# Overflow blocks of a mixture-of-experts layer moved behind their expert's first products, gathered two blocks and transposed one block ahead

## The chip, the cores and the metric

One core of one Trainium2 chip. The metric is the device time of one execution in microseconds (us), here the median of several.

## What is computed

One layer of a hybrid encoder trunk, 512 tokens of width 1024, float32: a mixer (gated DeltaNet beside chunked attention) and a layer norm, and then the part that the change is in, a mixture of 64 experts (gate-up weights 1024 x 512, down weights 256 x 1024) of which every token takes six, one shared expert, and a second layer norm:

```python
def moe_ffn(x, router_w, router_bias, w_gate_up, w_down, ws_gate_up, ws_down):
    scores = jax.nn.sigmoid((xt @ router_w).astype(jnp.float32))
    _, sel = lax.top_k(scores + router_bias.astype(jnp.float32), TOP_K)
    ...
    def block_fn(args):
        tok, wt, e = args
        gu = x_pad[tok] @ w_gate_up[e]
        h = jax.nn.silu(gu[:, :EXPERT_DIM]) * gu[:, EXPERT_DIM:]
        return (h @ w_down[e]) * wt[:, None]
    ...
    routed = jax.ops.segment_sum(y_rows.reshape(n_rows, D), row_tok, num_segments=N + 1)[:N]
    gus = xt @ ws_gate_up
    shared = (jax.nn.silu(gus[:, :SHARED_DIM]) * gus[:, SHARED_DIM:]) @ ws_down
    return (routed.astype(x.dtype) + shared).reshape(B, T, D)
```

## The kernel before

The phases before `experts_phase` (mixer, first layer norm, router, lists of tokens by expert) are not touched. `experts_phase` has one instruction stream per engine, tied by semaphores.

**Blocks.** Each expert works on a block of 64 token rows. Tokens beyond 64 of one expert go to overflow blocks of 64 rows, numbered j; `over_from` says which of them belong to which expert. How many there are depends on the data, so each engine reads two entries of `over_from` at each expert (`later_blocks`, L1622) and branches: `later(i, s)` is its overflow part, skipped or run once per block.

**Turns and steps.** A turn is 8 steps (`STEPS`), a step is one expert, e = 8i + s. There are 8 turns: the first and the last are written out, the six between are one hardware loop per engine (TensorE's is L1854). Step s of TensorE (`turn`):
- `later(i, s)`: overflow blocks of this expert;
- `gate_up(i, s)` (products L1765): 32 matmuls into bank `ps[k % 2]`, with k = s % 4 the weight buffer, incrementing `gu_psum[k]`;
- `transposes` (L1757): four transposes of gathered rows for a later pair of experts, into `ps[2]` or `ps[3]`, copied out by VectorE (L1911, `gathered_xT`);
- `down(i, s - 1)` (products L1772): the down products of the expert before, incrementing `y_psum`;
- `hidden(i, s)` (L1810): transpose of the hidden tile that ScalarE (silu, L1882) and VectorE (L1916) made, incrementing `h_psum[k]`.

In turn 0 the shared expert's down products (L1831) stand in the first four steps.

**One overflow block** (`later` of TensorE, L1778 to L1794), all in bank 5 (`shared`): wait for the expert's gate-up and down weights, for the scatter of the block before (`over_free`) and the gathered rows (`over_gathered`); eight products with the identity (L1786) that transpose `over_x`; VectorE copies them out (`over_xT`, L1924); gate-up products; silu on ScalarE (L1870), multiply on VectorE; transpose (L1792); copy on ScalarE (L1872); down products; ScalarE copies the result to `over_y` (L1875); GpSimd scatter-adds it (L1714) and gathers the next block's rows (L1696) as soon as the transposes have read this one's.

**Weights.** `wgu` and `wdn` have four buffers each: 2 MB of gate-up weights (two DMAs of 1024 KB) and 1 MB of down weights for an expert. The first four experts are loaded earlier. SP then issues, in this order and one behind the other: gate-up of buffer s once `gu_psum[s]` says that its products are done (L2067), down of buffer s - 1 once `y_psum[s - 1]` does (L2073).

Of the kernel before, what the change touches and what calls it, by code (L numbers as in the profile page):

```python
# [1541 lines left out]
def experts_phase(nc, mem, T, ps, x1_rows, sums, w_down, ln_g, ln_b, out):  # L1542
# [67 lines left out]
    blank_word = at("blank_word", [P, 1], "qkT", 1632)  # L1610
# [14 lines left out]
    with nc.Block() as block:  # L1625

        @block.sync
        def _(sp):
            with sp.Fori(1, NE // GROUP) as i:

                for s in range(GROUP + 1):
                    if s < GROUP:
                        T["load_gu"](sp, s, GROUP * i + s, lambda: sp.wait_ge(gu_psum[s], i))
# [21 lines left out]
        def _(pool):  # L1655
# [45 lines left out]
            def later(i, s, alone):  # L1701
                start, end = later_blocks(pool, i, s)
                with pool.If(start < end):
                    with pool.Fori(start, end) as j:
                        pool.wait_ge(over_xt_psum, j + 1)
                        gather_later(j + 1, j + 1)
# [3 lines left out]
                        pool.wait_ge(over_y, j + 1)  # L1710
                        nc.gpsimd.tensor_copy(col2_o[:, :], row_idx[:, bass.ds(j + NE, 1)]).then_inc(over_col2, 1)
                        pool.wait_ge(blank, 1)
                        pool.wait_ge(over_col2, j + 1)
# [17 lines left out]
            gather_later(0, 1, True)  # L1731
            turn(0, first=True)
# [3 lines left out]
            nc.gpsimd.memset(blank_word[:, :], 0.0).then_inc(over_added, 1)  # L1736
# [3 lines left out]
            pool.wait_ge(over_gathered, 16 * blocks + 16)  # L1740
# [6 lines left out]
        def _(pe):  # L1747
# [28 lines left out]
            def later(i, s):  # L1776
                start, end = later_blocks(pe, i, s)
                with pe.If(start < end):  # L1778
                    with pe.Fori(start, end) as j:
                        k, now = block_at(i, s)  # L1780
                        pe.wait_ge(gu_in[k], GU_PARTS * 16 * now)
                        pe.wait_ge(dn_in[k], 16 * now)
                        pe.wait_ge(over_free, 16 * j + 16)
                        pe.wait_ge(over_gathered, 16 * j + 16)
                        for c in range(KC):
                            mm = nc.tensor.matmul(shared[:, c * BLK:(c + 1) * BLK], xo[:, c * P:(c + 1) * P],  # L1786
                                                  ident[0:BLK, 0:BLK], start=True, stop=True)
                        mm.then_inc(over_xt_psum, 1)
                        pe.wait_ge(over_xt_ready, j + 1)
                        gate_up_products(shared, xoT, k, slice(0, BLK)).then_inc(over_gu_psum, 1)  # L1790
                        pe.wait_ge(over_h, j + 1)
                        nc.tensor.transpose(shared[:, 0:P], h_o[:, :], ident[:, :]).then_inc(over_h_psum, 1)  # L1792
                        pe.wait_ge(over_ht, j + 1)
                        down_products(shared, hT_o, k).then_inc(over_y_psum, 1)  # L1794

# [40 lines left out]
            def turn(i, first=False, last=False):  # L1836
                for s in range(STEPS):
                    later(i, s)
# [268 lines left out]
```

## Time and profile before

| | us |
|---|---|
| median of 3 runs | 1496.49 (1493.37 to 1501.87) |
| the profiled execution | 1497.2 |
| its span | 1495.5 |
| TensorE busy, of the span | 87% |
| mean clock granted to TensorE | 0.936 of full speed |
| experts phase, first gate-up product to last down product | 839.3 to 1454.7 |

The page gives an engine's busy time in tenths for 40 equal slices of the span, one digit a slice of 37.4 us; DMA is the mean busy share of 16 DMA engines. A saturated stretch reads slightly above 1. A row of the timeline has start, duration, engine, line, operation and count, and in brackets how long the engine stood idle before it and what it waited for. PE is TensorE's matmuls, PEld its weight loads, PEldq its instruction queue, SPq the queue of SyncE, which issues the weight loads. "issue" means that no cause in the profile explains the idle time.

### The profile page before, as it was taken

What the parts mean: (1) busy time and instruction counts of PE and PEld (TensorE: products, weight loads), DVE (VectorE), ACT (ScalarE), POOL (GpSimd) and SP (SyncE); (2) the same over time, 40 slices, a digit from 0 to 9 for tenths busy, and PEclk for the clock granted to TensorE, in tenths of its full rate; (3) what the DMA queues carried; (4) which work ended last, traced back from release to release, by engine and by line L of the source; (5) the groups of instructions that cost most, each with busy time, mean ns of one, the idle gap of its engine ahead of it and who ended that gap; (6) DMA issues with size and microseconds to landing.
All of it is one profiled execution on the core that took longest, in us unless ns stands there. A gap on an engine that the chain in (4) does not pass through costs nothing. (4 is left out here: it accounts for less than half of the span.)

```text
span 1495.5 us, 23252 instructions
## 1 busy us (share of the span) xinstructions
PE 1303.4 (87%) x8245; PEld 783.0 (52%) x8246; DVE 450.5 (30%) x892; ACT 309.7 (21%) x825; POOL 282.3 (19%) x355
## 2 busy tenths in 40 slices
PE   6999999999998988999999689978787958878680
PEld 5455556555653446888558445544444535444340
DVE  1545544554424442333248211111010101111006
ACT  1222333133312342222231001101011101111020
POOL 2201110111014202000000223323222313322132
PEclk8999999999998998999999899989888979989895
DMA  4441121124001204335821689999999996799874
GB/s 116 119 144 49 44 61 49 43 56 140 0 1 28 57 1 127 98 95 166 348 88 71 220 292 373 342 398 386 403 368 374 384 402 246 288 375 392 341 227 174
DMA packets 134583, 294.87 MB, mean 197 GB/s; under 512 B 12928, under 2 KB 82688, under 8 KB 117968
## 3 DMA queue, kind: packets, MB, share of 16 engines
q1 hardware_dynamic: 117824, 265.72, 47.6%
q0 software_dynamic: 15552, 25.46, 7.2%
q10 hardware_dynamic: 1104, 2.16, 0.4%
q8 instruction: 83, 1.36, 0.3%
q14 instruction: 20, 0.16, 0.0%
HBM read 278.57 MB, written 27.04 MB: 204 GB/s over the span
## 5 line engine op out<-in xcount | busy, mean ns | idle before, releaser
L1765 PE MATMUL bank<-expert_gu,gathered_xT 128*64 128x256 f32 x2048 | 250.8, 400 | 71.1 <-issue 56.0
L1765 PEld LDWEIGHTS bank<-expert_gu,gathered_xT 128*64 128x64 f32 x2048 | 167.4, 144 | 143.5 <-issue 81.2
L427 PE MATMUL bank<-xT,w_head 128*128 128x512 f32 x480 | 241.0, 612 | 1.2 <-PEq L85 1.2
L1916 DVE SCALAR_TENSOR_TENSOR hidden<-gate,slot_w,bank 128x128 f32<-128x128 f32 x64 | 22.2, 347 | 431.7 <-ACT gate L1882 431.7
L1772 PE MATMUL bank<-expert_down,hiddenT 128*64 128x512 f32 x512 | 123.9, 604 | 0.6 <-issue 0.6
L1685 POOL DMA_INDIRECT sum_rows<-expert_y,row_col x64 | 101.4, 1584 | 49.4 <-POOL row_col L1680 47.0
L427 PEld LDWEIGHTS bank<-xT,w_head 128*128 128x128 f32 x480 | 78.8, 190 | 48.5 <-issue 42.4
L1882 ACT ACTIVATE gate<-bank 128x128 f32<-128x128 f32 x64 | 17.8, 278 | 317.6 <-PE bank L1765 317.6
L605 POOL TENSOR_TENSOR LO<-LT_diagonal,level_blocks 128x256 f32<-128x256 f32 x48 | 38.2, 829 | 233.1 <-DVE LT_corner L771 233.1
L1402 DVE TENSOR_TENSOR w_lo<-w_tile,w_hi 128x1024 fp32r<-128x1024 f32 (+1 forms) x32 | 35.2, 1101 | 116.4 <-ACT w_hi L1302 116.4
L1680 POOL COPY row_col<-row_idx 128x1 int32 (+1 forms) x64 | 12.3, 192 | 293.4 <-ACT expert_y L1888 289.5
L1888 ACT COPY expert_y<-bank 128x512 f32<-128x512 f32 x63 | 36.9, 586 | 137.7 <-PE bank L1772 137.7
L1202 PE MATMUL bank<-xh,w_hi 128*128 128x512 f32 x128 | 51.0, 399 | 9.1 <-DVE w_lo L1402 9.1
L1772 PEld LDWEIGHTS bank<-expert_down,hiddenT 128*64 128x64 f32 x512 | 31.5, 136 | 47.6 <-issue 47.4
L717 DVE SCALAR_TENSOR_TENSOR by_channel<-bank,head_taps,by_channel 128x511 f32<-128x511 f32 (+2 forms) x72 | 53.9, 748 | 2.3
L1302 ACT CAST w_hi<-w_tile 128x1024 fp32r<-128x1024 f32 (+1 forms) x32 | 30.3, 946 | 117.1 <-PE bank L1202 110.5
L1202 PE MATMUL bank<-xl,w_hi 128*128 128x512 f32 x128 | 50.8, 397 | 0.0
L1202 PE MATMUL bank<-xh,w_lo 128*128 128x512 f32 x128 | 50.7, 396 | 0.0
L1757 PE MATMUL bank<-ident,gathered_x 128*128 128x128 f32 x256 | 42.6, 291 | 8.4 <-PEq L85 8.4
L1383 POOL COPY tok_col<-tok_idx 128x1 int32<-128x1 int32 x4 | 0.8, 192 | 255.5 <-DVE tok_idx L1532 255.4
L1911 DVE COPY gathered_xT<-bank 128x512 f32<-128x512 f32 x64 | 43.9, 686 | 8.9 <-PE bank L1757 8.9
L1757 PEld LDWEIGHTS bank<-ident,gathered_x 128*128 128x128 f32 x256 | 27.6, 143 | 32.4 <-issue 32.4
(325 smaller groups left out, 1911.0 us busy)
## 6 DMA issues: line engine op xcount, KB each, us to landing
expert_gu<-in_expert_w_gate_up_dram SPq DMA_DIRECT2D x128, 1024.0 KB
expert_down<-in_expert_w_down_dram SPq DMA_DIRECT2D x64, 1024.0 KB
w_head<-in_w_in_dram SPq DMA_DIRECT2D x32, 512.0 KB, 3.9
w_tile<-in_w_in_dram SPq DMA_DIRECT2D x16, 512.0 KB, 4.0
sum_rows<-zero_rows SPq DMA_DIRECT2D x2, 2048.0 KB, 11.7
w_tile<-in_w_branch_a_dram SPq DMA_DIRECT2D x8, 512.0 KB, 5.7
w_pair<-in_w_in_dram SPq DMA_DIRECT2D x6, 512.0 KB
x_rows<-in_x_dram SPq DMA_DIRECT2D x4, 512.0 KB
```

The lines of the kernel that those rows point to most:

```text
L427: mm = nc.tensor.matmul(bank[:, :], w_head[:, g, c, :], xT[:, c, :], start=(c == 0), stop=(c == KC - 1))
L605: nc.gpsimd.tensor_tensor(LO[:, l, :, :], LTd[:, :, :], all_packed(level[:, l, :]), ALU.mult).then_inc(loff_ready[l], 1)
L717: nc.vector.scalar_tensor_tensor(out=ch[:, g, k:SEQ], in0=bank[:, 0:SEQ - k], scalar=w, in1=ch[:, g, k:SEQ], op0=ALU.mult, op1=ALU.add).th ...
L1202: mm = nc.tensor.matmul(ps[4 * p + k][:, :], w[:, c, :].bitcast(F32R), x[:, c, :].bitcast(F32R), start=(c == 0 and part == 0), stop=(c == ...
L1302: nc.scalar.copy(w_hi[:, k % 2, 0:n, :].bitcast(F32R), w_t[:, k * KC:k * KC + n, :]).then_inc(hi_ready[p][k], 1)
L1402: nc.vector.tensor_tensor(w_lo[:, k % 2, 0:n, :].bitcast(F32R), w_t[:, k * KC:k * KC + n, :], w_hi[:, k % 2, 0:n, :], ALU.subtract).then_i ...
L1685: nc.gpsimd.indirect_dma_start(out=sums[s % 2][:, :], out_offset=bass.IndirectOffsetOnAxis(ap=col2[:, k:k + 1], axis=0), in_=y[:, k, :], i ...
L1757: mm = nc.tensor.transpose(ps[2 + a][:, c * P:(c + 1) * P], xg[:, q, chunk * P:(chunk + 1) * P], ident[:, :])
L1765: mm = nc.tensor.matmul(bank[parts[a], 0:2 * P], x[:, c, part], halves[:, a, :, :], start=(c == 0), stop=(c == KC - 1))
L1772: mm = nc.tensor.matmul(bank[parts[a], :], hidden_t[:, c * BLK:(c + 1) * BLK], wdn[k][:, c, a * (D // 2):(a + 1) * (D // 2)], start=(c == ...
L1888: nc.scalar.copy(y[:, b, :], ps[6 + b % 2][:, :]).then_inc(y_ready[b], 1)
L1911: nc.vector.tensor_copy(xgT[:, q % 2, a * KC // 2:(a + 1) * KC // 2, :], ps[2 + a][:, :].rearrange("p (c n) -> p c n", n=P)).then_inc(xt_r ...
```

## The change

1. TensorE runs `later` behind `gate_up` and `transposes` of the same step instead of ahead of them; ScalarE behind its silu of the step, VectorE behind its multiply and its copy of the step. The wait for gate-up weights in `later` goes, since `gate_up` has made it; the wait for down weights moves to the down products.
2. The transposes of block j + 1 are made inside block j, between gate-up and the hidden transpose, in bank 2 or 3, whichever the step leaves free; VectorE copies them at the end of its part. Block 0's are made in the first step. The first of the eight stays a product with the identity, the others become transposes.
3. GpSimd gathers two blocks ahead: rows of blocks 0 and 1 ahead of turn 0, then block j + 2 inside block j.
4. TensorE does not wait for `over_free` (the scatter) any more, but for `over_y` (ScalarE's copy).
5. SP reloads a gate-up buffer at `h_psum[s]` (hidden transpose) instead of `gu_psum[s]`, since the overflow products now read it after the expert's own.
6. `over_y` and `over_col2` count one more from the start.

```diff
@@ sync
-                        T["load_gu"](sp, s, GROUP * i + s, lambda: sp.wait_ge(gu_psum[s], i))
+                        T["load_gu"](sp, s, GROUP * i + s, lambda: sp.wait_ge(h_psum[s], i))
@@ gpsimd
-                        pool.wait_ge(over_xt_psum, j + 1)
-                        gather_later(j + 1, j + 1)
+                        pool.wait_ge(over_xt_psum, j + 2)
+                        gather_later(j + 2, j + 2)
...
             gather_later(0, 1, True)
+            nc.gpsimd.memset(blank_word[:, 1:2], 0.0).then_inc(over_y, 1)
+            nc.gpsimd.memset(blank_word[:, 2:3], 0.0).then_inc(over_col2, 1)
+            pool.wait_ge(over_xt_psum, 1)
+            gather_later(1, 1)
             turn(0, first=True)
@@ tensor
+            def over_transposes(bank):
+                nc.tensor.matmul(bank[:, 0:BLK], xo[:, 0:P], ident[0:BLK, 0:BLK], start=True, stop=True)
+                for c in range(1, KC):
+                    mm = nc.tensor.transpose(bank[:, c * BLK:(c + 1) * BLK], xo[:, c * P:(c + 1) * P], ident[0:BLK, 0:BLK])
+                mm.then_inc(over_xt_psum, 1)
...
                     with pe.Fori(start, end) as j:
-                        k, now = block_at(i, s)
-                        pe.wait_ge(gu_in[k], GU_PARTS * 16 * now)
-                        pe.wait_ge(dn_in[k], 16 * now)
-                        pe.wait_ge(over_free, 16 * j + 16)
-                        pe.wait_ge(over_gathered, 16 * j + 16)
-                        for c in range(KC):
-                            mm = nc.tensor.matmul(shared[:, c * BLK:(c + 1) * BLK], xo[:, c * P:(c + 1) * P],
-                                                  ident[0:BLK, 0:BLK], start=True, stop=True)
-                        mm.then_inc(over_xt_psum, 1)
+                        pe.wait_ge(over_y, j + 1)
                         pe.wait_ge(over_xt_ready, j + 1)
                         gate_up_products(shared, xoT, k, slice(0, BLK)).then_inc(over_gu_psum, 1)
+                        pe.wait_ge(xt_ready[2 * (q % PAIRS) + a], i + (q // PAIRS + 1))
+                        pe.wait_ge(over_gathered, 16 * j + 32)
+                        over_transposes(ps[2 + a])
                         pe.wait_ge(over_h, j + 1)
                         nc.tensor.transpose(shared[:, 0:P], h_o[:, :], ident[:, :]).then_inc(over_h_psum, 1)
+                        pe.wait_ge(dn_in[k], 16 * now)
                         pe.wait_ge(over_ht, j + 1)
                         down_products(shared, hT_o, k).then_inc(over_y_psum, 1)
+                        pe.wait_ge(over_xt_ready, j + 2)
@@ tensor, turn
-                    later(i, s)
...
                         transposes(i + q // PAIRS, q % PAIRS, s % 2)
+                    if first and s == 0:
+                        pe.wait_ge(over_gathered, 16)
+                        over_transposes(shared)
+                    later(i, s, last)
```

The queue of TensorE in one step of the loop, before (`expert_gu_2333` and `expert_down_2337` are the buffers of this expert, `expert_down_2336` that of the expert before; TENSOR_LOAD and ISA read the bounds of the overflow loop, COMPARE_AND_BRANCH skips it):

```order
L1778 COMPARE_AND_BRANCH
L1779 UNCONDITIONAL_BRANCH
...
L1786 MATMUL bank<-ident,over_x 128x64 x8
...
L1765 MATMUL bank<-expert_gu_2333,over_xT 64x256 x16
L1792 MATMUL bank<-ident,over_hidden 128x128
L1772 MATMUL bank<-expert_down_2337,over_hiddenT 64x512 x4
...
L1765 MATMUL bank<-expert_gu_2333,gathered_xT 64x256 x16
L1757 MATMUL bank<-ident,gathered_x 128x128 x4
...
L1772 MATMUL bank<-expert_down_2336,hiddenT 64x512 x4
L1810 MATMUL bank<-ident,hidden 128x128
```

And the same step now:

```order
L1769 MATMUL bank<-expert_gu_2333,gathered_xT 64x256 x16
L1761 MATMUL bank<-ident,gathered_x 128x128 x4
L1622 TENSOR_LOAD over_from
...
L1791 COMPARE_AND_BRANCH
...
L1769 MATMUL bank<-expert_gu_2333,over_xT 64x256 x16
L1797 ISA
L1781 MATMUL bank<-ident,over_x 128x64
L1783 MATMUL bank<-ident,over_x 128x64 x7
L1800 MATMUL bank<-ident,over_hidden 128x128
...
L1776 MATMUL bank<-expert_down_2337,over_hiddenT 64x512 x4
...
L1776 MATMUL bank<-expert_down_2336,hiddenT 64x512 x4
L1820 MATMUL bank<-ident,hidden 128x128
```

The expert's own gate-up and the usual transposes now stand ahead of the register loads, the branch and the block, and the other expert's down products behind them.

## Rows read from the trace of the kernel before

**Rows 1.** The page, busy tenths of the DMA engines in 40 slices

```profile
DMA  4441121124001204335821689999999996799874
```

**Rows 2.** Windows: length, busy of PE, PEld, DVE, ACT, POOL; clock, DMA share, GB/s

```profile
893.00:1443.00 550.00, 451.50 (x2986) 254.53 (x2984) 61.41 (x128) 66.72 (x192) 155.07 (x193) 0.90 0.96 362
944.00:1102.00 158.00, 126.98 (x829) 71.56 (x827) 17.64 (x37) 18.83 (x55) 44.62 (x56) 0.89 1.03 392
1234.00:1242.00 8.00, 7.64 (x53) 3.81 (x53) 0.95 (x2) 1.13 (x3) 1.76 (x2) 1.00 0.39 140
1250.00:1262.00 12.00, 10.74 (x78) 5.45 (x76) 1.29 (x3) 2.16 (x6) 2.21 (x4) 1.00 0.41 118
1278.00:1290.00 12.00, 11.64 (x86) 6.30 (x85) 0.95 (x2) 1.89 (x5) 3.56 (x4) 1.00 0.28 90
1412.00:1422.00 10.00, 9.25 (x62) 4.60 (x64) 1.31 (x3) 1.88 (x5) 1.94 (x3) 1.00 0.50 163
1442.00:1444.00 2.00, 2.00 (x20) 1.50 (x18) 0.00 (x0) 0.09 (x1) 1.16 (x1) 1.00 0.38 58
```

**Rows 3.** Timeline of TensorE, one step without overflow block

```profile
1167.12 3.67 PE L1765 MATMUL bank<-expert_gu,gathered_xT 128*64 128x256 f32 x32
1170.72 0.66 PE L1757 MATMUL bank<-ident,gathered_x 128*128 128x128 f32 x4
1171.31 1.94 PE L1772 MATMUL bank<-expert_down,hiddenT 128*64 128x512 f32 x8
1173.18 0.33 PE L1810 MATMUL bank<-ident,hidden 128*128 128x128 f32 x1
```

**Rows 4.** Timeline of the first overflow block, ahead of expert 7

```profile
905.07 1.97 PE L1786 MATMUL bank<-ident,over_x 64*128 64x64 f32 x16
...
907.07 0.69 DVE L1924 COPY over_xT<-bank 128x512 f32<-128x512 f32 x1 [3.41 <-PE bank L1786]
...
907.82 5.22 PE L1765 MATMUL bank<-expert_gu,over_xT 128*64 128x256 f32 x32 [0.78 <-DVE over_xT L1924]
...
913.53 0.35 DVE L1916 SCALAR_TENSOR_TENSOR over_hidden<-over_gate,slot_w,bank 128x128 f32<-128x128 f32 x1 [5.77 <-ACT over_gate L1870]
...
913.93 0.33 PE L1792 MATMUL bank<-ident,over_hidden 128*128 128x128 f32 x1 [0.90 <-DVE over_hidden L1916]
...
914.62 1.94 PE L1772 MATMUL bank<-expert_down,over_hiddenT 128*64 128x512 f32 x8 [0.35 <-ACT over_hiddenT L1872]
...
916.38 1.47 PE L1765 MATMUL bank<-expert_gu,gathered_xT 128*64 128x256 f32 x12
```

**Rows 5.** Timeline of SP, reloads of buffers 0 and 1 around expert 41

```profile
1219.49 21.61 SPq L2067 DMA_DIRECT2D expert_gu<-in_expert_w_gate_up_dram  x4
```

**Rows 6.** Waits of TensorE: us in total, times, longest

```profile
PE bank L1786 <- DMA expert_down<-in_expert_w_down_dram: 16.9, 3, 10.2
```

**Rows 7.** The first product after a jump, and two branches of TensorE's queue (min/median/max ns)

```profile
995.61 0.70 PE L1765 MATMUL bank<-expert_gu,gathered_xT 128*64 128x256 f32 x2 [10.69 <-issue]
...
L1854 PEldq COMPARE_BRANCH  x6: 86/6106/6449, 983.1 to 1368.8; - x6
...
L1778 PEldq COMPARE_BRANCH  x63: 70/245/4230, 849.5 to 1445.9; - x63
```

**Rows 8.** Timeline of GpSimd's first gather; landing of the load issued beside it

```profile
839.03 1.01 POOL L1696 DMA_INDIRECT over_x<-x_rows,over_tok_col  x1 [0.78 <-PE bank L1757]
...
over_y<-x_rows POOLq DMA_DIRECT2D x1, 256.0 KB, 8.5
```

**Rows 9.** Timeline of TensorE, the last product

```profile
1452.77 1.94 PE L1772 MATMUL bank<-expert_down,hiddenT 128*64 128x512 f32 x8 [0.63 <-issue]
```

**Rows 10.** Gate-up products of the overflow blocks, ns min/median/max, 893 to 1455 us

```profile
L1765 PE MATMUL bank<-expert_gu,over_xT x224: 379/606/689, 907.8 to 1411.1; 128*64 128x256 f32 x112
```

**Rows 11.** TensorE's queue in the step of rows 3: down's wait, register loads

```profile
L1818 PEldq EVENT_SEMAPHORE  x1: 51/51/51, 1168.9 to 1168.9; - x1
...
L1622 PEldq TENSOR_LOAD <-over_from x2: 325/328/330, 1171.6 to 1172.5; - x2
```

More of the change, by code:

```diff
@@ L1609, in experts_phase @@
     odd_sums = T["xT"][:, :, :].rearrange("p (t a) n -> p t (a n)", t=TT)
-    blank_word = at("blank_word", [P, 1], "qkT", 1632)
+    blank_word = at("blank_word", [P, 3], "qkT", 1632)
     g_row, b_row = at("ln2_g_row", [P, D], "w_t"), at("ln2_b_row", [P, D], "w_t", 4096)
@@ L1709, in later @@
                             pool.wait_ge(scattered[before], 16 * then_)
-                        pool.wait_ge(over_y, j + 1)
+                        pool.wait_ge(over_y, j + 2)
                         nc.gpsimd.tensor_copy(col2_o[:, :], row_idx[:, bass.ds(j + NE, 1)]).then_inc(over_col2, 1)
                         pool.wait_ge(blank, 1)
-                        pool.wait_ge(over_col2, j + 1)
+                        pool.wait_ge(over_col2, j + 2)
                         nc.gpsimd.indirect_dma_start(
@@ L1735, in _ @@
             turn(TURNS - 1, last=True)
-            nc.gpsimd.memset(blank_word[:, :], 0.0).then_inc(over_added, 1)
+            nc.gpsimd.memset(blank_word[:, 0:1], 0.0).then_inc(over_added, 1)
             scatter(TURNS - 1, STEPS - 1, last=True)
@@ L1739, in _ @@
             pool.wait_ge(over_free, 16 * blocks + 16)
-            pool.wait_ge(over_gathered, 16 * blocks + 16)
+            pool.wait_ge(over_gathered, 16 * blocks + 32)
             pool.wait_ge(sd_done, 2 * TT)
@@ L1774, in down_products, with later @@
                 return mm
-            def later(i, s):
+            def over_transposes(bank):
[3 more added lines that the diff above has]
+                mm.then_inc(over_xt_psum, 1)
+            def later(i, s, last=False):
+                k, now = block_at(i, s)
+                a = (s + 1) % 2
+                q = (s - 1) // 2 if last and s == STEPS - 1 else (s + 1) // 2
                 start, end = later_blocks(pe, i, s)
@@ L1878, in turn @@
                 for s in range(STEPS):
-                    later(i, s)
                     k, now = block_at(i, s)
@@ L1882, in turn @@
                     nc.scalar.activation(gate[:, k % 2, :], ps[k % 2][:, 0:P], ACT.Silu).then_inc(gate_ready[k], 1)
+                    later(i, s)
                     if not (first and s == 0):
@@ L1917, in weighted, with copy_over_x @@
                                                       op0=ALU.mult, op1=ALU.mult)
+            def copy_over_x(bank):
+                nc.vector.tensor_copy(xoT[:, :, :], bank[:, :].rearrange("p (c n) -> p c n", n=BLK)).then_inc(over_xt_ready, 1)
             def later(i, s):
@@ L1922, in later @@
                     with dve.Fori(start, end) as j:
-                        dve.wait_ge(over_xt_psum, j + 1)
-                        nc.vector.tensor_copy(xoT[:, :, :], shared[:, :].rearrange("p (c n) -> p c n", n=BLK)) \
-                            .then_inc(over_xt_ready, 1)
                         dve.wait_ge(over_gate, j + 1)
                         weighted(h_o[:, :], gate_o[:, :], shared[:, P:2 * P], j + NE).then_inc(over_h, 1)
+                        dve.wait_ge(over_xt_psum, j + 2)
+                        copy_over_x(ps[2 + (s + 1) % 2])
             def turn(i, first=False, last=False):
                 for s in range(STEPS):
-                    later(i, s)
                     k, now = block_at(i, s)
@@ L1937, in turn @@
                         copy_x(i + q // PAIRS, q % PAIRS, s % 2)
+                    if first and s == 0:
+                        dve.wait_ge(over_xt_psum, 1)
+                        copy_over_x(shared)
+                    later(i, s)
                     if first and s < TT:
```

## Prediction

> **What bounds the kernel now.** I read the busy tenths first. From slice 24 (893 us) on, the DMA row of [rows 1] stands at 9 but for a 6 and a 7 (1234 to 1309 us) and the end: the last part of the kernel streams 64 experts' weights through four buffers. So the time from 893 us on is the time that the 16 DMA engines need, plus what they stand dry.
>
> The stretches of [rows 2] put numbers on both. Saturated, the DMA share reads 1.03 (944 to 1102 us). Over 893 to 1443 us it reads 0.96: 0.07 / 1.03 x 550 = 37 us dry, which rounding leaves uncertain by 3. The four largest dry stretches, by (1.03 - share) / 1.03 x length, are 5.0 us at 1234, 7.2 at 1250, 8.7 at 1278 and 5.1 at 1412: 26.0 us; the rest is short ones. I take 35 us dry in all, so 515 us of moving. That is 9.2 us for each of the 56 experts loaded in this time (8 to 63). Where nothing stands dry I reckon with 9.1.
>
> TensorE's own step, without overflow, is 6.4 us: 3.67 of gate-up, 0.6 of transposes, 1.9 of down, 0.33 for the hidden transpose [rows 3]. That is shorter than 9.1, so TensorE ought to wait for weights at every expert, yet they stand dry. The reason is the overflow blocks. [rows 4] show the first of seven (experts 7, 9, 27, 41, 42, 44 and 58 have one), before expert 7: transposes 1.97, a wait for VectorE's copy, gate-up products 5.22, a wait, the hidden transpose, a wait, down 1.94; expert 7's own products start 11.3 us after the block began. During that time no buffer comes free. Each dry stretch begins when the loads already issued are through, and ends when SP issues the next: the SP row [rows 5] spans 1219.5 to 1241.1 us, the gap over expert 41's block.
>
> Two more things hold TensorE. Three of the blocks waited 16.9 us for down weights, one of them 10.2 [rows 6], with the expert's own products, which need no down weights, queued behind. And at the jumps back of the turn loop (five, ahead of experts 16, 24, 32, 40 and 48) TensorE stands up to 10.7 us with "issue" as cause: the loop's branch takes 6.1 us in the median, and the longest skip over an unused overflow body 4.23 us where the median is 0.245 [rows 7]. I read the two as the parts of the 10.7: 10.7 - 4.2 - 1.5 for the register loads between them [rows 11] leaves about 5 for the jump.
>
> **The change, part by part.** *Order in a step.* The block moves from before gate_up(s) to behind transposes(s), and its transposes are made one block ahead, between its gate-up and its hidden transpose. The new block costs TensorE: gate-up 3.6 (x32 at full clock, as in [rows 3]); transposes 1.2 (the first stays a product of two passes, 2 x 1.97 / 16 = 0.25; seven become transposes of one pass, for which the nearest rows are the four of 0.66 in [rows 3], so 7 x 0.15 at most); hidden transpose 0.33, a wait of 0.35 for ScalarE's copy, down 1.94 [rows 4]. Sum 7.4 us. The silu and the multiply need 0.9 us from the end of the products to the hidden transpose (913.04 to 913.93, [rows 4]); the 1.2 us of transposes cover that. VectorE's 0.69 us copy lies behind it, beside the down products. Block: 11.3 becomes 7.4, or 11.0 if the products run at the lower clock (below). GpSimd gathers two blocks ahead; its waits for scatters stay on its own queue, and the wait of TensorE for over_free, which cost nothing that a row shows, goes: zero.
>
> *The down wait* moves behind 3.7 + 0.6 + 3.6 + 1.2 = 9.1 us of work. Of expert 58's 10.2 us about 1 is left, and the others vanish.
>
> *The jump.* gate_up no longer stands behind the load of two registers and the skip branch. The branch of up to 4.23 us now runs beside 4.3 us of gate-up and transposes (more at the lower clock after a stall). The stall at a jump falls from 10.7 us to 5.3 at best; kept whole it is the upper bound.
>
> *What it adds.* SP may reload a gate-up buffer only after h_psum, not gu_psum: 0.6 + 1.9 + 0.33 = 2.8 us later [rows 3]. On SP the down load of the expert before is queued behind it and goes out 0.3 to 0.5 us later. Every fourth gate-up load already stood behind a down load, and loses only 0.35. While the DMA has a backlog this costs nothing; the cover is gone where it is dry, and then the delay is paid once per dry stretch.
>
> *At the start* step 0 gains 1.2 us of transposes and a wait for the first gather. It is issued at 839.03 and the load beside it takes 8.5 us to land [rows 8], so it may land at 847.5, against 845.2 when TensorE is there: 0 to 2.3 us, I take 1.3. Turn 0 is bound by TensorE, so the 2.5 us count in full. Two memsets and one gather on GpSimd precede turn 0; the gather queued behind them is needed seven steps later.
>
> *What stays dry.* A step with a block now lasts 6.4 + 7.4 = 13.8 us. For experts 41, 42 and 44 the reloads come 13.8, 6.4, 13.8 apart: 34 us for three loads of 9.1, so 7 us must come from backlog; [rows 5] with [rows 2] show that after loads issued by 1220 the DMA share was low only from 1234 to 1242 on, some 15 us of backlog, enough. For 7 and 9 there is no backlog: five loads of 9.1 against TensorE's 4 x 6.4 + 2 x 7.4 + 6.4 = 47, 1.3 dry, and the later release 2.8. With one more us at jumps and rounding I take 6 us (bounds: 1, all covered; 16, if blocks take 9.5 and the jump stall stays).
>
> *The end.* The weights end at about 1443, where the share falls to 0.38 [rows 2], TensorE at 1454.7 [rows 9]: 11.7 us behind, since the six experts from 58 on ran at their own pace after a late block. Now TensorE has caught up: behind the last down weights come at least 2 us of down products, at most a step of 6.4 + 1.9. I take 4.5.
>
> **Sum**, against the profiled execution (1497.2 us, span 1495.5): + 2.5 at the start, - (35 - 6) of dry time, - (11.7 - 4.5) at the end = - 33.7, so 1463.5 us. That execution is 0.7 us above the median of the runs shown, far inside what a measurement of this kernel can tell from no change (about 0.5%, 7.5 us).
>
> **A rule weighed.** The over products ran at 606 ns in the median, 379 at best, the mark of the lower clock level (1.2 against 2.4 GHz; the mean clock granted here is 0.90 [rows 2]), for most of their number [rows 10]; ahead of each TensorE had made narrow 64-column products and then waited for a copy. Now full products stand right ahead, so I take the 379 level. The Trainium skill (TensorE: Matmul & The Clock Gate, Part 4) says that transpose-mode work does not count as busy for the clock; by it the seven new transposes would bring the low level more often. In the usual step, four of them run at full clock [rows 3], which does not bear it out. What it would give is rival 1.
>
> **The rivals.** *1. The block stays long.* The clock falls around it anyway, and products and transposes take up to twice as long: 11.0 us. That adds 3.6 us to each block; hidden for 27 and 58, which have backlog, and paid at the other five less what backlog covers: about 16 us. Time: 1463.5 + 16 = 1479.5. For it: the low level follows every pause so far. Against: the pause ahead of the products is gone.
>
> *2. The later release eats it.* If the DMA is dry at each of the five jumps and seven blocks when the load is released, 12 x 2.8 = 33 us come back: 1497, no change. Against: the DMA was saturated for 158 us on end [rows 2], through two jumps.
>
> *3. The skip branch (slower).* It now stands between transposes(s) and down(s-1). The queue is past the transposes 1.8 us after gate-up starts (1168.9 against 1167.12), and the register loads take 1.5 us (two loads of 0.33, 1171.6 to 1172.5, each followed by 0.5 to 0.6 of checks) [rows 11]: the branch begins at 3.3 and has 1.0 us before down is due. With its usual 0.25 nothing is held; from 1.0 us on down is. If it took 4.2 us at every expert, as after a jump, each step would be 3.2 longer, 9.6 us: TensorE alone would need 56 x 9.6 + 7 x 7.4 + 5 x 5.3 = 616 us where this part now takes 562 (893 to 1455). Time: 1497 + 54 = 1551, and no change where the branch takes 3.2 (3.2 - 1.0 = 2.2 us, 56 times, is what the shorter blocks, jumps and step leave). Against: 0.245 is the median of 63 [rows 7], the skip now jumps over less (nine passes of transposes instead of sixteen), and it is as far from its target as before. The Trainium skill (Runtime: NRT & Kernel Launch, Instruction fetch mechanics) says that a taken branch to a page outside the window waits for a DMA fetch; by that rule the layout of the new code decides, and nothing here shows it.
>
> **Chances.** The forecast (1452 to 1472, from residual dry 1 to 10 and an end of 2 to 8) 0.58; rival 1 and its mild forms (1472 to 1488) 0.27; rival 2 0.07; rival 3 or a milder slower form 0.05; 0.03 for another slow-down in which later release and low clock meet. Faster 0.85, same 0.07, slower 0.08. The range reaches from 1450 (dry time all gone, moving at 9.0 per expert) into rival 1, to 1484.
>
> **What would show it.** Right: DMA share near 1.03 from 944 to the end of the weights, 8 us dry or less; 7.4 us more for a step with a block, over products at 379 ns; jump stalls of 5 to 6 us; TensorE waiting for gate-up weights at many experts, as "DMA expert_gu"; the last down product at about 1421. Wrong: over products at 606 ns (rival 1); new short dry stretches that end with h_psum (rival 2); gaps ahead of down products (rival 3); a moving time above 9.2 us per expert.

## The result and the profile after

| | us |
|---|---|
| before, median of 4 runs | 1494.93 (1491.09 to 1501.87) |
| changed, median of 4 runs | 1449.22 (1447.05 to 1452.23) |
| ratio | 0.9691, 95% interval [0.9649, 0.9732] |
| forecast | 1463.5, range 1450 to 1484 |

The change is faster by 45.7 us. The sign was forecast, and so was the main mechanism, that the DMA's dry time goes; the size was not: the time lies 0.8 us below the low end of the range. The profiled execution took 1447.05 us, with a span of 1445.4, 50.1 less than the span before; the working below is against this pair.

The page of the changed kernel, the DMA's busy tenths and the queues. Against [rows 1] the dents at 1234 to 1309 us are gone:

```profile
DMA  4451111113100203333682169999999999999984
...
q8 instruction: 37, 0.61, 0.2%
```

The same queue on the page of the kernel before had more than twice the packets, a row that the prediction did not read:

```profile
q8 instruction: 83, 1.36, 0.3%
```

Windows of the changed kernel (columns as in [rows 2]). The share of the saturated stretch, 1.03, now holds from 893 to 1400 us, so what stands dry there is what rounding of the two shares hides, 5 us at most (0.01 / 1.03 x 507):

```profile
893.00:1400.00 507.00, 442.74 (x2984) 230.84 (x2982) 61.66 (x129) 67.88 (x196) 155.55 (x194) 0.93 1.03 391
944.00:1102.00 158.00, 136.20 (x918) 71.01 (x918) 19.04 (x40) 21.50 (x62) 49.64 (x63) 0.94 1.03 397
```

Timeline of TensorE, changed kernel, the step of expert 7 with the first overflow block, to be read against [rows 4]. The block (909.31 to 916.39) costs 7.1 us. All its products run at full clock, and so do the gate-up products of the other six blocks (3.67 us each; before, 3.67 to 6.57):

```profile
905.12 3.67 PE L1769 MATMUL bank<-expert_gu,gathered_xT 128*64 128x256 f32 x32
908.73 0.66 PE L1761 MATMUL bank<-ident,gathered_x 128*128 128x128 f32 x4
909.31 3.67 PE L1769 MATMUL bank<-expert_gu,over_xT 128*64 128x256 f32 x32
912.92 0.43 PE L1781 MATMUL bank<-ident,over_x 64*128 64x64 f32 x2
913.19 0.59 PE L1783 MATMUL bank<-ident,over_x 64*128 64x64 f32 x7
913.88 0.33 PE L1800 MATMUL bank<-ident,over_hidden 128*128 128x128 f32 x1
914.65 1.94 PE L1776 MATMUL bank<-expert_down,over_hiddenT 128*64 128x512 f32 x8 [0.45 <-ACT over_hiddenT L1885]
916.39 1.92 PE L1776 MATMUL bank<-expert_down,hiddenT 128*64 128x512 f32 x8
```

TensorE's queue in the changed kernel, the jump of the turn loop and the skip branch (min/median/max ns), against [rows 7]. The jump takes 0.214 us in the median where it took 6.106:

```profile
L1867 PEldq COMPARE_BRANCH  x6: 83/214/224, 974.4 to 1335.0; - x6
```

```profile
L1791 PEldq COMPARE_BRANCH  x64: 65/214/418, 845.2 to 1399.6; - x64
```

Waits of the changed kernel from 850 to 1445 us, where [rows 6] had 16.9 us for down weights, and the timeline row of the first product after the first jump, where [rows 7] had 10.69 "issue". What TensorE waits for now is the next weights:

```profile
PE bank L1769 <- DMA expert_gu<-in_expert_w_gate_up_dram: 59.3, 19, 8.7
```

```profile
979.90 5.36 PE L1769 MATMUL bank<-expert_gu,gathered_xT 128*64 128x256 f32 x32 [3.74 <-DMA expert_gu<-in_expert_w_gate_up_dram]
...
1404.12 1.94 PE L1776 MATMUL bank<-expert_down,hiddenT 128*64 128x512 f32 x8 [1.21 <-DMA expert_down<-in_expert_w_down_dram]
```

The second of these is the last product, 48.65 us earlier than in [rows 9]. The last down weights land at 1404.1 (before: 1444.0).

**Where the 50.1 us came from.** Expert 4's products start 0.2 us later than before (886.16 against 885.93). From there to the last landing it takes 40.1 us less. From that landing to the end of the last product it is 2.0 us instead of 10.7, 8.7 less. The tail behind it is 39.3 instead of 40.8, 1.5 less. Sum: -0.2 + 40.1 + 8.7 + 1.5 = 50.1.

### The profile page after: what moved, and what is told of

It is laid out like the page before. It is cut to its first block and busy times, and to the rows that moved or that the text cites. A ratio compares the mean times of both kernels' runs of the same rounds, so it can differ in the third digit from the quotient of the medians.

```text
span 1445.4 us, 23188 instructions
## 1 busy us (share of the span) xinstructions
PE 1287.2 (89%) x8205; PEld 753.1 (52%) x8206; DVE 449.9 (31%) x893; ACT 309.8 (21%) x825; POOL 283.9 (20%) x359
## 5 line engine op out<-in xcount | busy, mean ns | idle before, releaser
L1769 PE MATMUL bank<-expert_gu,gathered_xT 128*64 128x256 f32 x2048 | 262.4, 414 | 63.4 <-DMA expert_gu<-in_expert_w_gate_up_dram 59.3
L1769 PEld LDWEIGHTS bank<-expert_gu,gathered_xT 128*64 128x64 f32 x2048 | 156.3, 149 | 152.7 <-issue 43.9
## 6 DMA issues: line engine op xcount, KB each, us to landing
sum_rows<-zero_rows SPq DMA_DIRECT2D x2, 2048.0 KB, 11.7
```

Of the source, the lines that this page charges most:

```text
L1769: mm = nc.tensor.matmul(bank[parts[a], 0:2 * P], x[:, c, part], halves[:, a, :, :], start=(c == 0), stop=(c == KC - 1))
```

## The experiments

In profiled executions of these kernels the first expert starts anywhere from 837.5 to 843.1 us, with the same kernel at 837.46 in one and at 842.23 in another, and that is ahead of all that is studied. So beside the medians I give the interval from the first gate-up product of expert 0 to that of expert 63, and its parts by turn (experts 0 to 8, 8 to 16, and so on), read from the starts of these products on TensorE's timeline. For the two profiled executions of the changed kernel it is 559.44 and 559.36 us; no other kernel was profiled twice, so how far the interval varies is known from this pair alone. The medians come from four series of runs, and the kernel before had 1494.93 to 1497.15 us in them: medians of different series can differ by 2 us for that reason alone. "Short" and "long" tell how many instructions TensorE's turn loop has (counted in the program, a weights load and a product as one each).

| kernel | loop | 0-8 | 8-16 | 16-24 | 24-32 | 32-40 | 40-48 | 48-56 | 56-63 | interval | median |
|---|---|---|---|---|---|---|---|---|---|---|---|
| before | 1762 | 83.8 | 72.5 | 69.5 | 80.6 | 64.2 | 106.8 | 59.5 | 70.3 | 607.2 | 1494.93 |
| e1, before, short | 1650 | 81.2 | 61.2 | 72.1 | 72.8 | 69.5 | 92.4 | 67.4 | 69.0 | 585.6 | 1473.48 |
| e5, before, late release | 1762 | 85.3 | 73.6 | 70.5 | 83.1 | 63.9 | 104.8 | 60.5 | 70.9 | 612.6 | 1497.92 |
| e3, order only | 1760 | 81.8 | 66.8 | 72.8 | 73.1 | 71.4 | 106.0 | 66.9 | 66.2 | 605.0 | 1493.54 |
| e3b, order, short | 1648 | 81.3 | 64.4 | 71.4 | 68.3 | 74.6 | 93.1 | 68.3 | 63.4 | 584.8 | 1478.60 |
| e4, down wait first | 1657 | 80.9 | 62.4 | 71.5 | 70.1 | 72.8 | 80.5 | 70.1 | 62.2 | 570.5 | 1458.41 |
| e2, changed, long | 1769 | 83.7 | 63.6 | 73.0 | 70.7 | 73.8 | 81.3 | 67.4 | 55.9 | 569.3 | 1461.33 |
| e8, padded | 1785 | 81.0 | 62.5 | 72.6 | 71.4 | 73.8 | 80.1 | 68.6 | 55.6 | 565.5 | 1457.24 |
| e9, padded less, one run | 1721 | 81.0 | 62.9 | 72.8 | 71.0 | 73.2 | 80.0 | 69.2 | 55.9 | 566.0 | 1460.13 |
| e6, scatter wait | 1665 | 81.0 | 62.4 | 71.2 | 71.2 | 72.0 | 79.1 | 68.2 | 56.8 | 561.9 | 1456.61 |
| changed | 1657 | 81.0 | 61.4 | 72.5 | 71.7 | 71.3 | 73.4 | 72.4 | 55.6 | 559.4 | 1449.22 |
| e7, shared late | 1657 | 81.5 | 61.9 | 71.7 | 71.2 | 72.0 | 73.5 | 71.8 | 55.6 | 559.1 | 1450.04 |
| e10, shared in turn 2 | 1657 | 59.9 | 73.7 | 72.9 | 69.5 | 72.3 | 73.4 | 71.2 | 56.7 | 549.5 | 1443.37 |

A turn of about 73 us is 8 x 9.1: the DMA bounds it. The turn with the blocks of experts 41, 42 and 44 (40-48) alone gives 33.4 of the 47.8 us.

### e1: the old order with a shorter loop

```diff
-                        for c in range(KC):
-                            mm = nc.tensor.matmul(shared[:, c * BLK:(c + 1) * BLK], xo[:, c * P:(c + 1) * P],
-                                                  ident[0:BLK, 0:BLK], start=True, stop=True)
+                        nc.tensor.matmul(shared[:, 0:BLK], xo[:, 0:P], ident[0:BLK, 0:BLK], start=True, stop=True)
+                        for c in range(1, KC):
+                            mm = nc.tensor.transpose(shared[:, c * BLK:(c + 1) * BLK], xo[:, c * P:(c + 1) * P], ident[0:BLK, 0:BLK])
```

> The kernel before, its order untouched; of the eight transposing products of an overflow block the last seven become transposes of one pass, which leaves the turn loop of TensorE some 110 instructions shorter. Fit theory (the mis-sized term is the jump: the shorter loop is no longer fetched anew each turn): instruction-queue packets fall from 83 to about 37, the branch at a jump from 6.1 us to 0.2, the 10.7 us waits at a jump go, and with them a part of the 35 us dry: 10 to 25 us faster than before. Order theory (only the new order gains): packets stay near 83 and the jump at 6 us; seven blocks shorter by at most 0.9 us each, so 1 to 6 us faster.

Measured: 1473.48 us (1471.56 to 1478.60), ratio 0.9849 [0.9794, 0.9903]. The page has the 37 packets of the changed kernel, and the jump is a short branch:

```profile
q8 instruction: 37, 0.61, 0.2%
```

```profile
L1854 PEldq COMPARE_BRANCH  x6: 83/214/221, 977.5 to 1347.9; - x6
```

The 10 to 25 us of the fit theory are met, and the packets and the branch show that the shorter loop is kept in the old order too. The 21.4 us are not the price of the jump alone, though. The edit also shortens the blocks, by more than the 0.9 us each that was expected: on TensorE's timeline the seven sets of transposes take 7.6 us together (0.84 to 1.41 each) where they took 18.8 (1.97 to 3.64), and the gate-up products of four blocks run wholly at full clock, where it was one. No run separates the two in the old order.

The gain falls in turns 8-16 (-11.3), 24-32 (-7.8) and 40-48 (-14.4), while 16-24, 32-40 and 48-56 give 15.8 back. The waits for down weights grew from 16.9 us:

```profile
PE bank L1785 <- DMA expert_down<-in_expert_w_down_dram: 27.0, 3, 10.2
```

### e2: the changed kernel with the long loop

Its edit is that of e1 the other way round, in `over_transposes`: eight products, no transpose.

> The changed kernel with eight products in place of one product and seven transposes: the same order, the loop of TensorE as long as before. Fit theory: packets return to about 80, the branch at a jump to about 6 us, stalls of 5 to 8 us at five jumps; the DMA backlog hides most of it, so 2 to 12 us slower than the changed kernel (1451 to 1461 us). Order theory: packets stay at 37, jump at 0.2 us, and 7 x 0.8 us of longer blocks, mostly covered: 0 to 4 us slower.

Measured: 1461.33 us (1459.89 to 1462.78), ratio to before 0.9763 [0.9714, 0.9813]; 12.1 us slower than the changed kernel, at the upper end of what the fit theory gave. The packets are 83 again and the jump takes 5.954 us in the median. Part of it is not the jump: the step with the first block of e2 is 2.7 us longer (down products at half clock once, 3.40 instead of 1.94, and transposes of 2.00 instead of 1.02), the others 1.0.

### e8 and e9: instructions that are never executed

Since e2 also lengthens the block, these two lengthen the code and execute nothing more than one branch in each block. This is e8; e9 has `range(3)`:

```diff
                 with pe.If(start < end):
+                    with pe.If(end < start):
+                        for c in range(7):
+                            nc.tensor.transpose(shared[:, c * BLK:(c + 1) * BLK], xo[:, c * P:(c + 1) * P], ident[0:BLK, 0:BLK])
                     with pe.Fori(start, end) as j:
```

> The changed kernel with seven transposes per step in a branch that is never taken, inside the block's branch: nothing more is executed but a branch in each block, and the turn loop of TensorE grows by 128 instructions to about 1785. Fit theory: like the changed kernel with the long loop, packets about 83, jump 5 to 6 us, 8 to 14 us slower than the changed kernel (1457 to 1463). If that kernel was slower for its longer block transposes: within 3 us of the changed kernel, packets 37.

> The same with three transposes per step in the branch never taken: a loop of about 1721 instructions, between the 1657 that are kept and the 1762 that are fetched anew. Fit theory: all or nothing, so either packets 37 and 1449 us, or packets about 80 and about 1460; which of the two tells on which side of 1721 the bound lies. Against the theory would be packets and time in between.

Measured, e8: 1457.24 us (1456.52 to 1459.57), ratio to before 0.9744 [0.9728, 0.9760], all four runs above all eight of the changed kernel: 8.0 us slower, at the low edge of the 8 to 14. The blocks are no longer: six of the seven steps with a block take 13.4 us, as in the changed kernel. One run of e9 (a loop of 1721) took 1460.13, with the first expert as late as 843.1; its interval, 566.0, is that of e8. Both have the packets of the long loop and a jump of 6 us (page and queue of e8):

```profile
q8 instruction: 83, 1.36, 0.4%
```

```profile
L1870 PEldq COMPARE_BRANCH  x6: 86/6064/6191, 978.1 to 1343.0; - x6
```

```profile
1282.54 6.60 PE L1769 MATMUL bank<-expert_gu,gathered_xT 128*64 128x256 f32 x32 [4.86 <-issue]
```

So code that is never executed is enough to bring the fetches back, all or nothing: 37 packets at 1665 instructions (e6), 83 at 1721. The last row is e8 at the jump to expert 48: 4.86 us of waiting, then products at about half clock for 2.9 us more. At the jumps to experts 24 and 32 the wait for weights covers it, and turns 16 to 32 take the same time in both (144.0 and 144.2 us). The price falls in turn 40-48 (80.1 against 73.4): 1.8 us in expert 40's step, and 4.9 at expert 48, where the blocks have made TensorE late and the weights are already there. Turn 48-56 gives 3.8 us back, and the whole interval is 6.1 us longer. Beside e8, e2 is 4.1 us slower (3.8 in the interval), about what the longer transposes cost in the new order. The skip branch stays short even where the loop is fetched anew; in the kernel before it had once taken 4.230 (e8's queue):

```profile
L1791 PEldq COMPARE_BRANCH  x64: 70/278/449, 848.9 to 1409.4; - x64
```

### e3 and e3b: the new place without the look-ahead

`later` stands behind `transposes`, and the reload waits for `h_psum`, as in the change; the block makes its own transposes first and waits for down weights and scatter at its start, as before. e3b has the short form of e1.

> The kernel before with the block moved behind the transposes on all engines and the gate-up reload after the hidden transpose, but with the block's own transposes in place (eight products, no look-ahead) and its down wait at its start. Fit theory: the jump stall stays near 6 us (the branch is still fetched), block about 10 us, so about half of the gain: 15 to 30 us faster than before (1465 to 1480). Order theory: nearly the whole gain, 35 us or more (1460 or less), with packets still at 80. If neither order nor fit but only the look-ahead gains: within 10 us of before.

> The same as the run before (block moved, no look-ahead), with one product and seven transposes, so a short loop. Fit theory: packets about 37, no jump stall, and 8 to 20 us faster than the same order with the long loop. Order theory: at most 6 us between the two. What is left to the changed kernel (1449 us) is the look-ahead and the place of the down wait: 3 to 12 us.

Measured, e3: 1493.54 us (1489.77 to 1498.45, 10 runs), ratio 0.9985 [0.9957, 1.0013]. Both theories expected at least 15 us, and both miss: the new place, with the later release that it needs, gains nothing that can be measured. The third possibility that was named, within 10 us of before, holds. e3b: 1478.60 us (1477.07 to 1481.57), 0.9884 [0.9833, 0.9934], 15 us faster than e3 (kept loop and shorter transposes together, as in e1) and no faster than e1. Its interval (584.8) is that of e1 (585.6). In the profiled pair its first expert starts 4.5 us later (842.10 against 837.55), so the 5 us between the medians need not come from the edit.

What order alone leaves standing is seen in e3b's waits and in its first block, which VectorE's copy and multiply still stretch:

```profile
PE bank L1785 <- DMA expert_down<-in_expert_w_down_dram: 13.9, 3, 6.7
PE bank L1785 <- DMA sum_rows<-over_y,over_row_col: 4.0, 1, 4.0
```

```profile
914.31 3.67 PE L1765 MATMUL bank<-expert_gu,over_xT 128*64 128x256 f32 x32 [1.51 <-DVE over_xT L1924]
918.88 0.33 PE L1792 MATMUL bank<-ident,over_hidden 128*128 128x128 f32 x1 [0.89 <-DVE over_hidden L1916]
```

Its step with a block takes 15.67 us (907.74 to 923.41), that of the changed kernel 13.38.

### e4: the down wait back at the start of the block

```diff
                         pe.wait_ge(over_y, j + 1)
+                        pe.wait_ge(dn_in[k], 16 * now)
...
-                        pe.wait_ge(dn_in[k], 16 * now)
                         pe.wait_ge(over_ht, j + 1)
```

> The changed kernel with one line moved: TensorE waits for the expert's down weights at the start of the block, as before, not ahead of the down products. What separates the changed kernel (1449) from the same order without look-ahead (1479) is this wait and the look-ahead. Wait theory: where TensorE has caught up with the DMA (experts 27, 41, 42, 58) the wait stands 3 to 7 us ahead of the block, the products behind it run at the low clock, reloads come late: 10 to 22 us slower than the changed kernel (1459 to 1471). Look-ahead theory (the 2.3 us that the transposes in advance take off each block are the whole): 0 to 5 us slower.

Measured: 1458.41 us (1455.93 to 1462.38), ratio to before 0.9741 [0.9721, 0.9761]: 9.2 us slower than the changed kernel in the medians, 11.1 in the interval, about the low end of the wait theory and twice the other's. Waits of e4, and expert 58's block on its timeline, where 6.73 us of waiting are followed by 2.9 us of low clock:

```profile
PE bank L1769 <- DMA expert_down<-in_expert_w_down_dram: 14.1, 3, 6.7
```

```profile
1374.82 6.54 PE L1769 MATMUL bank<-expert_gu,over_xT 128*64 128x256 f32 x32 [6.73 <-DMA expert_down<-in_expert_w_down_dram]
```

In the changed kernel the same block waits 1.33 us, behind its products:

```profile
1366.71 3.57 PE L1776 MATMUL bank<-expert_down,over_hiddenT 128*64 128x512 f32 x8 [1.33 <-DMA expert_down<-in_expert_w_down_dram]
```

From e3b to e4 lies what the look-ahead and the missing scatter wait give together: 14.2 us in the interval, 20.2 in the medians.

### e5: the later release alone, in the kernel before

```diff
-                        T["load_gu"](sp, s, GROUP * i + s, lambda: sp.wait_ge(gu_psum[s], i))
+                        T["load_gu"](sp, s, GROUP * i + s, lambda: sp.wait_ge(h_psum[s], i))
```

> The kernel before with one edit: a gate-up buffer is reloaded after the hidden transpose (h_psum), 2.8 us later than after the gate-up products. In the kernel before the DMA stands dry at some of the seven blocks. Theory of the prediction (the delay is paid once per dry stretch, four large and some short): 4 x 2.8 to 7 x 2.8 us, so 8 to 20 us slower than before. Rival (short stretches are covered by the down load that goes out in between): within 4 us of before.

Measured: 1497.92 us (1494.31 to 1505.39, 10 runs) beside 1497.15 of before, ratio 1.0011 [0.9992, 1.0030]. In time that is -1.2 to +4.5 us, and excludes the 8 to 20 of my theory. The interval of the one profiled run is 5.4 us longer, but that run (1504.81) is among the two slowest of the ten. A small price is possible and not shown.

### e6: the scatter wait put back into the changed kernel

```diff
                         pe.wait_ge(over_y, j + 1)
+                        pe.wait_ge(over_free, 16 * j + 16)
```

> The changed kernel with the wait put back that the change in a few words names: at the start of a block TensorE waits for the scatter of the block before (over_free). Theory: the scatter of the block before is long done or its cost is hidden by the blocks being six or more steps apart, except 41, 42 and 44, one step apart: within 3 us of the changed kernel. Rival (the scatter is what TensorE waited for): the wait stands at expert 42's and 44's block, some 5 us each with the low clock behind it, and 6 to 15 us slower.

Measured: 1456.61 us (1454.73 to 1459.80) beside 1450.01 (1449.40 to 1454.24) of the changed kernel on the same chip (e11, below), ratios to before 0.9744 [0.9712, 0.9776] and 0.9693 [0.9664, 0.9722]. The rival is right in kind: there is one such wait in the whole run, at expert 42's block, on e6's timeline:

```profile
1228.24 5.36 PE L1769 MATMUL bank<-expert_gu,over_xT 128*64 128x256 f32 x32 [3.90 <-DMA sum_rows<-over_y,over_row_col]
```

The scatter that it waits for was issued at 1220.05. The trace gives the time from issue to landing for the scatter of expert 41's block, in e6 first and then in the kernel before ("DMA to landing"):

```profile
DMA to landing us min/median/max: 8.0/8.0/8.0
```

```profile
DMA to landing us min/median/max: 2.8/2.8/2.8
```

Before, it was issued at 1238.48, in the dry stretch of [rows 2] from 1234 to 1242 (share 0.39), and had landed ahead of the next block. Now it shares the DMA with the weights, and lands too late. It is not one case: the seven scatters of the changed kernel land 7.8 to 9.5 us after their issue, with a DMA share of 1.01 to 1.03 over each, those of the kernel before after 2.8 to 5.1, with 0.06 to 0.84.

With the low clock behind it the wait is 5.6 us at that place, and turn 40-48 is 5.7 longer than in the changed kernel. The later turns take a part back, and the whole interval is 2.5 longer. So the wait costs between 2.5 and 6.6 us; the intervals of the two ratios overlap, and no run here fixes it closer.

### e7, e10 and e11: what is left

If only the DMA bounds the rest, what is left is what it stands dry ahead of 893 us (share 0.79 from 840 to 893 in the changed kernel). In turn 0 the shared expert's down products make the first four steps 11.65 us long (the first one 13.75). e7 moves them to steps 4 to 7, e10 to turn 2, one in every second step. These are the main lines of e10 for TensorE; VectorE's follow them:

```diff
+            turn(1)
+            turn(2, adds=True)
-            with pe.Fori(1, TURNS - 1) as i:
+            with pe.Fori(3, TURNS - 1) as i:
...
-                    if first and s < TT:
-                        shared_down(s)
+                    if adds and s % 2 == 0:
+                        shared_down(s // 2)
```

> The changed kernel with the four shared down products of turn 0 made in steps 4 to 7 in place of 0 to 3. If from here on the time is what the DMA needs plus what it stands dry, then what is left dry is ahead of 893 us: steps 0 to 3 of 11.7 us become 6.3, the weights of experts 4 to 7 are asked for earlier, and of some 13 us dry there 8 to 12 go: 1437 to 1441 us. Rival (TensorE bound in turn 0, and the steps 4 to 7 that get longer give it back): within 3 us of the changed kernel.

> The changed kernel with the four shared down products taken out of turn 0 and made in turn 2 (experts 16, 18, 20, 22), where TensorE waits for weights anyway; turns 1 and 2 are written out for TensorE and VectorE in place of two passes of the loop. Moving them within turn 0 gained nothing, since TensorE had as much to do up to expert 9 as before. If the DMA bounds all the rest, then steps 0 to 3 of 6.3 us in place of 11.7 let the weights of experts 4 on be asked for 5.3 us earlier each, the 12 us that the DMA stands dry between 840 and 893 us go, and a pair of steps in turn 2 takes 18.0 us where the DMA needs 18.2: 9 to 13 us faster than the changed kernel (1436 to 1440). Rival (the gain is given back at turn 2, where a step of 11.7 us delays the reload, or the end is TensorE's from expert 56 on): within 4 us of it.

> The changed kernel itself, on the same chip as the three before, so that they are compared with it directly: 1449 us, within 3.

Measured, e7: 1450.04 us (1446.64 to 1452.26), interval 559.1: no gain, the rival. The dry time only moves, as two windows show (840 to 893 at 0.94, and then 893 to 930 at 0.82, where the changed kernel has 1.01):

```profile
840.00:893.00 53.00, 48.45 (x317) 24.79 (x315) 9.51 (x19) 5.98 (x18) 15.13 (x20) 0.99 0.94 343
893.00:930.00 37.00, 32.93 (x203) 16.53 (x203) 6.47 (x13) 4.22 (x12) 9.34 (x12) 1.00 0.82 300
```

e10: 1443.37 us (1440.41 to 1446.29, 5 runs), ratio to before 0.9654 [0.9626, 0.9682]; all five below all four of the changed kernel on the same chip (1450.01). That is 6.6 us less in the medians and 9.9 in the interval, the low end of the 9 to 13 or a little under it. Windows of e10:

```profile
840.00:893.00 53.00, 51.66 (x380) 28.34 (x378) 8.35 (x17) 7.02 (x21) 17.01 (x24) 0.97 0.94 340
893.00:1390.00 497.00, 435.14 (x2848) 222.99 (x2846) 64.50 (x131) 65.44 (x188) 148.66 (x186) 0.93 1.03 393
```

It is the fastest version of this study.

## Why the prediction was right and where it was wrong

**The jump, which failed.** The prediction said: "The stall at a jump falls from 10.7 us to 5.3 at best." It fell to nothing. The working behind it holds where the code is still fetched: in e8 the two jumps that no wait for weights covers stand 4.82 and 4.86 us. What failed is that I had treated these 5 us as a price that a jump of this loop has, whatever stands in it. It is the price of fetching the loop's code anew, and the change took 105 instructions out of the loop (seven transposes per step in place of two-pass products, less what it adds), which made it short enough to be kept. e1 shows with the old order that a short loop is kept, e8 that code which is never executed is enough to lose it. Its size here is 8.0 us in the medians (1457.24 - 1449.22) and 6.1 in the interval; with the jump as I had it the time lies inside the range. In the kernel before, the shorter loop and the shorter transposes give 21.4 us together (e1); what the jump alone costs there is not known. The row that would have told was on the page: 83 instruction packets, where a loop that is kept fetches nothing; and rival 3 gave the layout of the code a sign only for the worse.

**The rest of the 16.4 us.** The sum said -33.7 and the pair shows -50.1. Beside 6.1 for the jump, 5.0 are in the moving (below), 2.3 at the start, 1.5 at the end and 1.5 in the tail, which the sum left out. All have one sign, so nothing cancelled. Some of it is run to run: in the second profile of the changed kernel (e11) the end takes 3.4 us instead of 2.0 and the tail 41.0 instead of 39.3.

The Trainium skill (Runtime: NRT & Kernel Launch, Instruction fetch mechanics) gives TensorE's instruction memory 2048 instructions, filled in blocks of 256, and speaks of a window of two such blocks outside of which a taken branch must fetch. The runs agree that such a branch waits for a fetch. They do not agree with the window of two blocks: a loop of 1665 instructions, more than six blocks, jumps in 0.2 us. That one of 1721, less than 2048, does not is no clear case against the other number, since no run here varied how a loop lies on the borders of the blocks.

**The moving and the residual dry time.** 515 us of moving and 6 dry were forecast, 521 in all from 893 us; it was 511 (893 to 1404.1), 9.1 a load, with at most 5 of it dry by the share. So the 515 were 4 to 9 us too many. The GB/s column of [rows 2] would have been nearer: 362 x 550 / 392 = 508 us at the rate of the saturated stretch. With the jumps fetched (e8) the share of 893 to 1390 is 1.02; that is 5 us dry, but rounding allows 0 to 10, so whether the 6 were right for the kernel that I thought I had stays open.

**The end.** 4.5 us from landing to last product were forecast, 2.0 measured (3.4 in e11), where it was 10.7 and not 11.7 before. Right in kind.

**The start.** Step 0 grew by 2.05 us (13.75 against 11.70), forecast 2.5. In the pair, 1.8 of it is given back ahead of expert 0, which is run to run.

**The block.** 7.4 us forecast, 7.1 measured, and the clock as forecast: the over products ran at 379 ns in the median and 430 at most, where [rows 10] had 606. Rival 1 did not come. The low clock still follows most waits, 13 of the 19 for gate-up weights (5.36 us of products after 3.74 of waiting at expert 16, above), but the DMA does not wait for TensorE there. That the full clock comes from the full products right ahead, as I argued, is not shown: in e1, with the old order and transposes in place of products, the median is 379 ns too.

**The down wait.** Forecast: 10.2 us at expert 58 become 1, the others vanish. Measured: 1.33 there. Put back (e4), it costs 9 to 11 us.

**The scatter wait, priced at zero.** That was right for the kernel before and wrong for the changed one. e3, e3b and e6 wait 4.2, 4.0 and 3.9 us once each, and in e6 the wait costs 2.5 to 6.6 us. The prediction asked only what the wait cost in the trace. But the scatter was quick (2.8 us) because the DMA stood dry beside it, and the change takes just that away: with the DMA full it needs 8.0.

**The later release (rival 2).** It did not eat the gain; alone in the old kernel it costs at most 4.5 us by the runs' times (e5), not 8 to 20. The reason I did not test; the down load that goes out in between is one that fits.

**The skip branch (rival 3).** 0.214 us in the median, 0.418 at most, and 0.449 at most where the loop is fetched (e8). It held nothing.

**Which part gains.** The prediction did not split the gain between the block's new place and the look-ahead. e3 shows that the place with its later release is worth nothing measurable by itself. In medians, from before: short loop with shorter transposes 21.4 us faster (e1); with the new place 5.1 slower again, or 0.8 faster by the interval (e3b); with the look-ahead and without the scatter wait 20.2 faster (e4, 14.2 by the interval); with the late down wait 9.2 faster (11.1). The look-ahead was not tried in the old place.

## What to carry to other kernels

Before pricing a hardware loop's jump as fixed, count the loop's instructions and read the instruction-queue packets: an edit that shortens the code may gain more than the work it saves, and one that pads it may lose as much. Moving a block of work alone gained nothing here; what paid was to make its inputs ahead of it and to move each wait to the first instruction that needs what it waits for. A wait on a transfer that costs nothing while the DMA stands dry must be priced again for a DMA that is full. And work that one engine does in a stretch that it bounds is best moved to a stretch that another bounds (e10); moved inside its own stretch (e7) it gains nothing.

## What the runs showed of the hardware

- A turn loop of 1648 to 1665 TensorE instructions is fetched in its first pass and not in the five that follow: in the changed kernel the instruction queue has no packet between 971.6 and 1344.9 us. With 1721 to 1785 it fetches 46 packets of 16 KB more (83 against 37), 8 to 10 in each of the five.
- At a jump these fetches come one by one while the DMA is saturated: in the kernel before at 981.7, 987.3, 992.9 and 998.4 us, 5.6 apart, though each packet takes 0.9 to 1.0 us itself.
- The same scatter lands 2.8 us after its issue in a dry stretch (share 0.39), and after 8.0 beside full weight loads; all seven take 2.8 to 5.1 in the kernel before and 7.8 to 9.5 in the changed one.
- The part ahead of the experts phase varies by 5 us between executions of one kernel (837.46 and 842.23), as much as some of the edits here cost, while the interval behind it agrees within 0.1 us in the one pair that there is.
